# Expert projections of a fused transformer kernel: three single passes on split operands in place of one full-precision matmul, with GpSimd, batched one-hots and an earlier exponent

## The reference, cut to what matters

```python
q = (xc @ w_query).reshape(C, PEER_HEADS, 2, PEER_HALF)
sc = jnp.einsum('thpd,hpnd->thpn', q, sub_keys).astype(jnp.float32)
top_s, top_i = lax.top_k(sc, PEER_TOPK)
cand_s = (top_s[:, :, 0, :, None] + top_s[:, :, 1, None, :]).reshape(C, PEER_HEADS, PEER_TOPK * PEER_TOPK)
...
best_s, best_pos = lax.top_k(cand_s, PEER_TOPK)
experts = jnp.take_along_axis(cand_i, best_pos, axis=-1)
gates = jax.nn.softmax(best_s, axis=-1)
u = expert_down[experts]
vv = expert_up[experts]
act = jax.nn.gelu(jnp.einsum('cd,chkd->chk', xc, u).astype(jnp.float32), approximate=False)
w = (gates * act).astype(xc.dtype)
return jnp.einsum('chk,chkd->cd', w, vv)
```

## Time and profile before

| | |
|---|---|
| median of 3 runs | 1725.3 us (1718.38 to 1726.87) |
| the profiled execution | 1728.26 us, of it the span of the trace 1726.2 us |
| PE, DVE, ACT busy | 1564.6 us (91%), 1074.9 us (62%), 699.1 us (40%) |
| POOL busy | 5.8 us |
| mean granted TensorE clock | 0.955 |

### The profile page before, as it was taken

How to read it: one execution, slowest core, us unless ns; L and a number is a source line. 1 busy time by engine, 2 the same in 40 slices (tenths; PEclk the granted TensorE clock), 3 DMA queues, 4 the chain that set the end, 5 groups by cost and what they waited for, 6 DMA issues and landing times. The chain is left out here.

```text
span 1726.2 us, 28966 instructions
## 1 busy us (share of the span) xinstructions
PE 1564.6 (91%) x8809; PEld 1383.0 (80%) x8809; DVE 1074.9 (62%) x2752; ACT 699.1 (40%) x1526; POOL 5.8 (0%) x13
## 2 busy tenths in 40 slices
PE   2997789998998999999999999879999997869987
PEld 1664578887997888999999999779999997658885
DVE  3577457957997776666666666555555554266663
ACT  0343211113323443544444444346555554336552
POOL 0000000000000000000000000000000000000000
PEclk9998789999999999999999999989999999679997
DMA  6410043442224555555555555374444441075410
GB/s 246 164 38 1 2 160 111 153 153 75 92 90 142 194 191 188 194 184 182 194 184 182 194 184 183 127 261 135 151 152 137 134 139 45 1 250 165 121 26 25
DMA packets 162586, 239.33 MB, mean 139 GB/s; under 512 B 41808, under 2 KB 91472, under 8 KB 161488
## 3 DMA queue, kind: packets, MB, share of 16 engines
q1 hardware_dynamic: 162160, 238.34, 42.2%
q10 hardware_dynamic: 352, 0.07, 0.0%
HBM read 237.09 MB, written 1.28 MB: 138 GB/s over the span
## 5 line engine op out<-in xcount | busy, mean ns | idle before, releaser
L187 PE MATMUL experts_acc<-experts_uh,experts_wh 128*128 128x512 f32 x512 | 201.5, 394 | 5.7 <-DVE experts_ul L1579 5.7
L188 PE MATMUL experts_acc<-experts_ul,experts_wh 128*128 128x512 f32 x512 | 201.1, 393 | 0.0
L189 PE MATMUL experts_acc<-experts_uh,experts_wl 128*128 128x512 f32 x512 | 200.1, 391 | 0.0
L1132 PE MATMUL plain_u<-ffn_h,down_raw 128*128 128x256 f32 x832 | 192.1, 382 | 0.4 <-PEq L1217 0.4
L1552 ACT ACTIVATE experts_uh<-ffn_h 128x512 fp32r<-128x512 f32 x256 | 147.1, 624 | 83.7 <-PE experts_acc L189 79.1
L189 PE MATMUL projection<-hT_high,down_low 128*128 128x256 f32 x608 | 172.1, 283 | 0.0
L188 PE MATMUL projection<-hT_low,down_high 128*128 128x256 f32 x608 | 172.0, 283 | 0.0
L187 PE MATMUL projection<-hT_high,down_high 128*128 128x256 f32 x608 | 171.7, 282 | 0.0
L1132 PEld LDWEIGHTS plain_u<-ffn_h,down_raw 128*128 128x128 f32 x832 | 154.1, 192 | 19.5 <-issue 1.1
L1579 DVE TENSOR_TENSOR experts_ul<-ffn_h,experts_uh 128x512 fp32r<-128x512 f32 x256 | 164.7, 684 | 3.0 <-ACT experts_uh L1552 3.0
L187 PE MATMUL mix_a_pj<-mix_a_wh,hT_high 128*128 128x384 f32 x384 | 136.8, 356 | 17.0 <-DVE mix_a_wl L560 17.0
(11 more groups left out here) (274 smaller groups left out, 3014.9 us busy)
## 6 DMA issues: line engine op xcount, KB each, us to landing
down_raw<-in_downT SPq DMA_DIRECT2D x256, 256.0 KB, 3.4
ffn_h<-in_up SPq DMA_DIRECT2D x256, 256.0 KB, 2.8
mix_a_w_raw<-in_wa SPq DMA_DIRECT2D x48, 768.0 KB, 5.9
block_w_raw<-in_w SPq DMA_DIRECT2D x16, 768.0 KB, 6.6
mix_b_w_raw<-in_wb SPq DMA_DIRECT2D x16, 768.0 KB, 6.7
route_raw<-in_route SPq DMA_DIRECT2D x16, 576.0 KB, 3.7
wo<-in_wo SPq DMA_DIRECT2D x2, 2048.0 KB, 10.4
mix_a_w_raw<-in_wa SPq DMA_DIRECT2D x16, 256.0 KB, 3.3
```

The lines of the kernel that those rows point to most:

```text
L187: pe.matmul(out, lhs[0], rhs[0], start=start, stop=False, skip_group_check=True)
L188: pe.matmul(out, lhs[0], rhs[1], start=False, stop=False, skip_group_check=True)
L189: return pe.matmul(out, lhs[1], rhs[0], start=False, stop=stop, skip_group_check=True)
L1132: mm = pe.matmul(self.u[b][:, 0:SEQ], self.raw[b][:, k, :], self.h[:, k, :], start=k == 0, stop=k == KD - 1, skip_group_check=True)
```

## The change

1. The 52 chunks projected ahead use the three passes as well (`Ahead` for `Plain`). ScalarE makes the high halves (two ACTIVATE of 128 x 512 for a chunk), GpSimd the low halves (two TENSOR_TENSOR of 128 x 512), and the next load into a raw buffer waits for the low half in place of the matmul. In the route phase the split of chunk n + 2 stands ahead of the GELU of chunk n in ScalarE's program, in the spread phase behind it.
2. The gates' exponent stands after 20 of the 28 chunks, not after all.
3. The indices are made in the other order (i2 first), and i1 is split into a coarse digit (of 16) and a fine digit (of 8), which are transposed in its place. `a1` is made as the product of two small one-hots, which are made for 8 groups at once: three TENSOR_TENSOR for 8 groups, and one of 128 x 512 for each group in place of four TENSOR_SCALAR.
4. The spread phase begins with `LEAD` = 8 more steps of projection ahead of the first group, and 2.875 in place of 3 steps for each group.

```diff
+BEFORE_GATE = 20
+LEAD = 8
+FINE = 8
...
     def load(self, sp, n, b):
         for h in range(2):
-            k = slice(KD // 2 * h, KD // 2 * (h + 1))
-            wait(sp, self.projected, n * 2 + (h - 3))
-            sp.dma_start(self.raw[b][:, k], self.down[n][:, k]).then_inc(self.landed[b][h], 16)
+            wait(sp, self.lows, n * 2 + (h - 3))
+            sp.dma_start(self.raw[b][:, self.half(h)], self.down[n][:, self.half(h)]).then_inc(self.landed[b][h], 16)
+
+    def split_high(self, act, n, b):
+        for h in range(2):
+            act.wait_ge(self.landed[b][h], (n - b) * 8 + 16)
+            wait(act, self.projected, n * 2 + (h - 3))
+            act.activation(self.high[b][:, self.half(h)], self.raw[b][:, self.half(h)], ACT.Copy).then_inc(self.highs, 1)
+
+    def split_low(self, pool, n, b):
+        for h in range(2):
+            k = self.half(h)
+            pool.wait_ge(self.highs, n * 2 + (h + 1))
+            pool.tensor_tensor(self.low[b][:, k], self.raw[b][:, k], self.high[b][:, k].bitcast(F32),
+                               ALU.subtract).then_inc(self.lows, 1)
...
         if k % (KD // 2) == 0:
-            pe.wait_ge(self.landed[b][k // (KD // 2)], (n - b) * 8 + 16)
+            pe.wait_ge(self.lows, n * 2 + (k // (KD // 2) + 1))
         if k == 0:
             wait(pe, self.done, n - 1)
-        mm = pe.matmul(self.u[b][:, 0:SEQ], self.raw[b][:, k, :], self.h[:, k, :], start=k == 0, stop=k == KD - 1,
-                       skip_group_check=True)
+        mm = three_passes(pe, self.u[b][:, 0:SEQ], [v[b][:, k, :] for v in (self.high, self.low)],
+                          [v[:, k, :] for v in self.hT], k == 0, k == KD - 1)
...
+            def early_chunk(n, b):
+                ahead.split_high(act, n + 2, b)
+                ahead.gelu(act, n, b, early[:, n, :])
+            over_chunks(act, 0, BEFORE_GATE, early_chunk)
             act.wait_ge(shifted_ready, 1)
             act.activation(gate[:], shifted[:], ACT.Exp).then_inc(gate_exp, 1)
+            over_chunks(act, BEFORE_GATE, EARLY, early_chunk)
...
+            dve.tensor_scalar(eighth[:], index[0][:], 1.0 / FINE, -0.5 + 0.5 / FINE, ALU.mult, ALU.add)
+            dve.drain()
+            dve.tensor_scalar(eighth[:], eighth[:], WHOLE, None, ALU.add)
+            dve.drain()
+            dve.tensor_scalar(coarse[:], eighth[:], -WHOLE, None, ALU.add).then_inc(cols_ready, 1)
+            dve.drain()
+            dve.scalar_tensor_tensor(fine[:], coarse[:], -float(FINE), index[0][:], ALU.mult, ALU.add).then_inc(cols_ready, 1)
...
+    def steps_by(g):
+        return LEAD + (STEPS - LEAD) * (g + 1) // GROUPS if g >= 0 else 0
+    joins = [min(next(g for g in range(GROUPS) if steps_by(g) >= (n + 1) * KD) + 2, GROUPS) for n in range(LATE)]
...
+                if g % BATCH == 0:
+                    digits(g // BATCH)
+                q = slice(g % BATCH * Q, g % BATCH * Q + Q)
                 wait(dve, g_ready, g - 1)
-                for q in range(Q):
-                    col = slice(g * Q + q, g * Q + q + 1)
-                    last = dve.tensor_scalar(a1[b][:, q, :], iota[:], slotT["i1"][:, col], slotT["gate"][:, col],
-                                             ALU.is_equal, ALU.mult)
-                last.then_inc(a1_ready, 1)
+                dve.tensor_tensor(a1[b][:].rearrange("p q (h l) -> p q h l", l=FINE),
+                                  coarse_of[:, q].unsqueeze(3).broadcast_to([P, Q, COARSE, FINE]),
+                                  fine_of[:, q].unsqueeze(2).broadcast_to([P, Q, COARSE, FINE]), ALU.mult).then_inc(a1_ready, 1)
...
+                if c + 2 < READY:
+                    ahead.split_high(act, c + 2, c % 2)
```

More of the change, by code:

```diff
@@ L1146, with __init__ @@
 class Projections:
[L1150 to L1153, removed]
+    def __init__(self, nc, ctx, ahead):
+        self.down, self.hT, self.raw, self.high, self.low = ahead.down, ahead.hT, ahead.raw, ahead.high, ahead.low
         self.u = [ctx.enter_context(nc.psum_tensor(f"projection{b}", [P, 512], F32)) for b in range(2)]
@@ L1208, in over_chunks, with route_phase @@
             one(i * 2 + b, b)
[L1211 removed]
+def route_phase(nc, weights, hT, sbt, slots, raw, landed, early, ahead):
     HP = 2 * HEADS_P
@@ L1256, in _ @@
                     sp.dma_start(raw[b][:], weights[i * NW + b + NW]).then_inc(landed[b], 16)
-            over_chunks(sp, 2, EARLY + 2, lambda n, b: plain.load(sp, n, b))
+            over_chunks(sp, 2, EARLY + 2, lambda n, b: ahead.load(sp, n, b))
+        @block.gpsimd
+        def _(pool):
+            over_chunks(pool, 0, EARLY + 2, lambda n, b: ahead.split_low(pool, n, b))
         def steps(eng, one):
@@ L1274, in one @@
                 for k in range(KD):
-                    mm = pe.matmul(qp[b % 2][:, 0:SEQ], raw[b][:, k, :], plain.h[:, k, :], start=k == 0, stop=k == KD - 1,
+                    mm = pe.matmul(qp[b % 2][:, 0:SEQ], raw[b][:, k, :], ahead.h[:, k, :], start=k == 0, stop=k == KD - 1,
                                    skip_group_check=True)
@@ L1289, in _ @@
             scores_of(HP - 1, NW - 1)
-            over_chunks(pe, 0, EARLY, lambda n, b: plain.project(pe, n, b))
-            for n, src in enumerate((index[0], index[1], gate)):
+            over_chunks(pe, 0, EARLY, lambda n, b: ahead.project(pe, n, b))
+            for n, src in enumerate((index[1], coarse, fine, gate)):
                 pe.wait_ge(cols_ready, n + 1)
@@ L1346, in _ @@
             dve.drain()
-            dve.tensor_scalar(part[:], pos[:], 4, None, ALU.logical_shift_right).then_inc(shifted_ready, 1)
+            dve.tensor_scalar(part[:], pos[:], TOPK - 1, None, ALU.bitwise_and).then_inc(shifted_ready, 1)
             dve.drain()
-            for half in range(2):
-                if half == 1:
-                    dve.tensor_scalar(part[:], pos[:], TOPK - 1, None, ALU.bitwise_and)
+            for half in (1, 0):
+                if half == 0:
+                    dve.tensor_scalar(part[:], pos[:], 4, None, ALU.logical_shift_right)
                     dve.drain()
@@ L1377, in _, with spread_phase @@
             last.then_inc(cols_ready, 1)
-def spread_phase(nc, slots, iota, early, spread, plain):
+def spread_phase(nc, slots, iota, early, spread, ahead):
     Q = 4
@@ L1452, in _ @@
             for g in range(GROUPS):
-                for m in range(STEPS * g // GROUPS, STEPS * (g + 1) // GROUPS):
+                for m in range(steps_by(g - 1), steps_by(g)):
                     n = EARLY + m // KD
-                    plain.step(pe, n, n % 2, m % KD)
+                    ahead.step(pe, n, n % 2, m % KD)
                 pe.wait_ge(a1_ready, g + 1)
```

74 lines of the change are left out of this document (49 added, 25 removed).

## The result

| | before | after |
|---|---|---|
| median of 4 runs | 1722.5 us (1718.4 to 1726.9) | 1765.2 us (1758.9 to 1770.2) |
| ratio | | 1.0246, 95% interval 1.0200 to 1.0291 |
| span of the profiled run | 1726.2 us | 1757.1 us |

What follows compares the result with a forecast made beforehand. TensorE was taken as the bound, with a 3.3 us gap at the seam. Terms -18.3, +1.7 and +0.1 made -16.5 us: 1728.3 to 1711.8, and 1709 as the profiled run stood 3 us above the median; range 1697 to 1742.

Steps and rivals of the forecast that it cites:

- its first rival: Both phases: reading GpSimd instructions and VectorE's two-input ones take turns; +12 us, median 1737 (1724 to 1750), chance 0.32.
- -4: Rival's route phase: taking turns from 340 on, PE ends near 387, VectorE first copies near 389, -4 us.
- +1.7: Spread phase's start: VectorE's first copy to first product takes 4.7 us instead of 3.03, +1.7 us.
- the ten steps ahead of it: Spread phase's start: 10 projection steps ahead of the first product, 3.6 us, hide under VectorE's 4.7 us.
- +14: Rival's spread phase: two-input work and subtractions packed 147 us, 163 with one blocked one-hot more a chunk: 155, +14.
- The passes in the route phase: Route phase: 28 chunks of 2.87 us from 291.3 end at 371.7, not 388.2; -16.5 us.
- The subtraction at 1.17 us: GpSimd's low halves: 1.17 us each, between 0.53 and 1.38; two a chunk keep up with PE's 2.87.
- ScalarE's exponent: Route phase: after chunk 19 the exponent and table loads cause one 1.5 us PE stall; its input is ready, no wait.
- The seam and start: Seam: VectorE's first copy at 374.6 against 392.85, -18.3 us; then 4.7 us to the spread phase's first product.
- The ring, 12.5: Spread phase: PE waits 0.57 us for late chunks' low halves, for each of 22 chunks, +12.5 us.
- The digits, 6.4: Spread phase: digits made once in 8 groups make PE wait 1.3 us, seven times, less overlap with ring waits: +6.4.
- Loads: nothing: Both phases: loads wait for the low half rather than the matmul, start earlier, and cost nothing.

Runs made afterwards that it cites:

- run 5: Changed kernel with GpSimd's subtraction replaced by two memsets (1.2 us a half, reading nothing), GpSimd's loop and ScalarE's last route-phase loop written out: 1709.3 us, ratio 0.9942.
- run 2: Changed kernel with ScalarE's last eight route-phase chunks written out, so that tables are loaded once: 1761.4 us, ratio 1.0224 to the kernel before.
- run 1: Changed kernel with GpSimd's subtraction replaced by three memsets (1.55 us a half, reading nothing), GpSimd's loop written out: 1730.1 us, ratio 1.0049.
- run 7: Changed kernel with passes and GpSimd subtractions in the spread phase alone, route-phase chunks in plain float32, ScalarE's loop written out at its end: 1759.8 us, ratio 1.0231.
- run 8: Kernel before with the exponent six chunks early and the first 8 route-phase chunks in three passes with GpSimd's subtractions: 1711.4 us, ratio 0.9951.
- run 9: Kernel before with the exponent six chunks early and the first sixteen route-phase chunks in three passes with GpSimd's subtractions: 1708.8 us, ratio 0.9947.
- run 3: Kernel before with only the gates' exponent moved to behind 20 chunks, the last 8 written out: 1715.6 us, ratio 0.9972.
- run 6: Changed kernel with passes and GpSimd subtractions in the route phase alone, spread-phase chunks in plain float32, ScalarE's last eight route-phase chunks written out: 1734.5 us, ratio 1.0082.
- run 4: Changed kernel without passes and split: chunks in plain float32, no GpSimd work; early exponent, digits and ten steps ahead kept: 1726.2 us, ratio 1.0033 to the kernel before.

## Why the prediction was wrong

**What failed: the choice between the forecast and its first rival.** The forecast let a GpSimd subtraction and VectorE's two-input work run at once. The rival had the mechanism: the two take turns. The Trainium skill (SBUF — State Buffer, Who interferes with whom) states it, and these runs agree: with a reading GpSimd instruction a one-hot takes 1.02 us on average, with a writing one 0.68. With that one thing taken away (run 5) the kernel runs at 1709.3 us. That this is the forecast's own number is partly luck: the forecast stood 16.5 us under the kernel before, run 5 stands 10.0 us under it by the ratio, and the kernel before ran faster beside run 5 (1720.2) than at the time of the forecast (1725.3). The forecast gave the rival 0.32, because no row could show it; but no row spoke against it either, and the memset of the earlier trace rows said nothing on reads.

**The rival's price was too low in both places,** 1737 for 1765, +12 us for +43, and so the range ended short.
- *Route phase, "-4".* It counted the 2.29 us index instructions from 340 on. Left out were the sixteen candidate sums at 297 to 347: at 0.42 us each they looked like nothing, but beside GpSimd each took 1.35, 14.9 us more in all, two thirds of VectorE's lateness. And it took PE's chunks to end last. They ended near 383; VectorE, 391.8, did. The first product came 5.6 us later than before, not 2.3 earlier (-4 and +1.7). Of these, 1.0 us is that the ten steps ahead of it, which were to hide (3.6 us under 4.7), took 5.6 at the lower clock.
- *Spread phase, "+14".* It packed the two engines' work without a gap and added one blocked one-hot a chunk. The phase takes 34.8 us longer than before, and of them 28.8 over run 5. VectorE is busy 38.6 us longer, since a one-hot waits for a whole subtraction of 1.26 us or more, and what stands behind it goes late; PE, idle in pieces, then fell to a clock of 0.92 (12.9 us). The forecast had no clock term.

**The forecast's other steps,** checked in run 5, where they are undisturbed:
- *The passes in the route phase* (to 371.7 without the stall, which run 5's written-out loop doesn't have): the first transpose is at 372.2. Right.
- *The subtraction at 1.17 us*: 1.26 at the least. The estimate of 1.20 that the forecast worked out from the 4497 ns in the Trainium skill (GPSIMD Engine Reference, section 3.1) was nearer; the trace agrees within 5%.
- *ScalarE's exponent*: the stall of 1.5 us became 5.9 in the change, because VectorE's input was late. The step "it doesn't wait" failed as a result of the first error.
- *The seam and start*: VectorE's first copy at 374.6 and 4.7 us to the first product; measured 375.65 and 4.85. Right within 1.1 us.
- *The ring, 12.5*: 6.3 us of waits, 12 times. *The digits, 6.4*: 8.9 us, 6 times. Together 15.2 for 18.9. But the phase took 147.1 us, not 141.2. PE's own records make 130.4 us where 122.3 was worked out, though an undisturbed group is as worked out (starts at 382.54 and 384.51, 1.97 us). Part of it is that after a stop the first matmul takes 0.36 us or more rather than 0.28; what the rest is stays open.
- *Loads: nothing*, since they would start earlier. In run 5 PE's chunks end on time, so right there. In the change the low halves are late, and the loads behind them: ScalarE's copies waited 12.0 us for them between 291 and 400 (and its table loads 3.4 more), and 23.2 in run 2, against 4.4 in run 5. VectorE was later than that, so it didn't set the end.

Not foreseen: a phase ends for all engines at once, so that work for the next phase which GpSimd finishes last holds PE (4.3 and 4.5 us in runs 1 and 7). In the change VectorE was later still, and PE waited 0.45 us there, as in the kernel before.

## What to carry to other kernels

Before work is moved to GpSimd, list VectorE's two-input instructions in the same stretch, however short (and the short one-input ones that the rows below name), for each may come to wait for a whole GpSimd instruction. Where a mechanism is stated and no row can show it, price it from its shortest, most frequent victims and let the range reach that far. Such work is free only where VectorE has slack: with 8 and 16 chunks' worth the first product came 4.6 and 7.2 us earlier here (runs 8 and 9 against 3), with 28 it came 5.1 later (run 6 against 4). Batching small instructions can lose as well, though it saves VectorE's time: run 4 did.

## What the runs showed of the hardware

- Beside GpSimd's subtraction VectorE's 128x256 sum went from 0.42 to up to 1.52 us, and GpSimd's instruction from 1.26 to up to 3.34. A 128x256 TENSOR_SCALAR and a CAST of one input went from 0.29 to 1.32 and 1.23. Maxima, searches and reductions, with one input, kept their times.
- A GpSimd memset left two-input instructions alone but could stretch these one-input ones (TENSOR_SCALAR and CAST of 128x256, 0.29 us alone): beside memsets they took 0.29 to 0.62 us in run 1 and 0.31 to 0.72 in run 5. The longest, which took 0.29 in the change with GpSimd idle there:

```profile
L1408 DVE TENSOR_SCALAR route_eighth<-route_eighth 128x256 f32<-128x256 f32 x1 | 0.7, 720 | 0.1
```

- The blocks behind the experts, in code that no run changes, differed in granted clock from run to run (0.91 or 0.96 over a stretch of 200 us), worth 8 to 10 us of a profile.
